# Four transformer layers on one core: the first four weight units taken by halves, with the products of the low weights last

## What is computed

```python
hn = rmsnorm(h, norm_mix[0])                  # h = x, [256, 1024]
q, k, v = split(hn @ w_qkv, 3)                # w_qkv [1024, 3072]; 8 heads of 128 channels
a = softmax(q0 k0^T * s + alibi) - lam * softmax(q1 k1^T * s + alibi)
o = rmsnorm(a @ v, subln) * (1 - lam_init)    # h = h + o @ w_o, then a SwiGLU FFN and a gated side input
```

## Time and profile before

| | us |
|---|---|
| median of 3 runs | 1311.12 (1311.06 to 1311.26) |
| the profiled execution | 1310.98 |
| its span, first to last instruction | 1309.2 |
| PE busy in it | 1299.0 (99%) |
| ACT busy | 847.5 (65%) |
| DVE busy | 963.5 (74%) |
| POOL busy | 114.8 (9%) |
| 16 DMA engines, bytes | 255.27 MB |

### The profile page before, as it was taken

The page is one execution under the profiler, slowest core; times in us unless marked ns, Lnnn a source line. Parts: engine busy times, 40 slices in busy tenths (PEclk is TensorE's granted clock), DMA queues, the critical chain, the costliest instruction groups (busy, mean ns, idle before and its releaser), DMA issues.

```text
span 1309.2 us, 20022 instructions
## 1 busy us (share of the span) xinstructions
PE 1299.0 (99%) x6642; PEld 1082.7 (83%) x6642; DVE 963.5 (74%) x1661; ACT 847.5 (65%) x1459; POOL 114.8 (9%) x163
## 2 busy tenths in 40 slices
PE   9999999999999999999999999999999999999998
PEld 7988888888888788888888888888887778888887
DVE  7877777676898676666699876666677887666664
ACT  7666666656788666665677666666578666666654
POOL 4020233410000000000010000000002210000000
PEclk9999999999999999999999999999999999999999
DMA  9454788876497556667647656676655545666661
GB/s 339 143 163 132 229 241 240 240 227 201 164 233 202 153 183 210 209 209 218 204 145 206 179 183 191 211 212 206 207 163 184 175 130 166 196 207 212 209 225 49
DMA packets 205055, 255.27 MB, mean 195 GB/s; under 512 B 72962, under 2 KB 163249, under 8 KB 204992
## 3 DMA queue, kind: packets, MB, share of 16 engines
q1 hardware_dynamic: 201984, 245.42, 60.6%
q0 software_dynamic: 2832, 8.49, 2.8%
q10 hardware_dynamic: 176, 0.54, 0.2%
HBM read 238.33 MB, written 1.13 MB: 183 GB/s over the span
## 4 chain that ended last, share of the span: by engine, by line
PE 93%; DVE 3%; ACT 1%; issue 1%; DMA 1%; POOL 0%; SPq 0%; DVEq 0%; ACTq 0%
PE acc L1620 15%; PE acc L1622 14%; PE acc L1621 14%; PE sc L1622 12%; PE sc L1620 12%; PE sc L1621 12%; PE turn L1781 3%; PE acc L1731 3%; PE acc L1733 3%; PE acc L1732 3%; PE turn L1883 1%; PE sc L1834 1%; DVE wlo L1139 1%; DVE z L1239 1%; PE turn L1863 1%
## 5 line engine op out<-in xcount | busy, mean ns | idle before, releaser
L829 ACT ACTIVATE whi<-raw,aT_gain 128x512 fp32r<-128x512 f32 (+2 forms) x612 | 403.8, 719 | 79.5 <-PE sc L1622 53.4
L1139 DVE SCALAR_TENSOR_TENSOR wlo<-raw,aT_gain,whi 128x512 fp32r<-128x512 f32 (+2 forms) x612 | 433.7, 764 | 28.6 <-ACT whi L829 24.5
L1620 PE MATMUL sc<-whi,xhi 128*128 128x512 f32 x640 | 249.4, 390 | 0.0
L1622 PE MATMUL sc<-whi,xlo 128*128 128x512 f32 x640 | 249.0, 389 | 0.0
L1621 PE MATMUL sc<-wlo,xhi 128*128 128x512 f32 x640 | 249.0, 389 | 0.0
L1620 PE MATMUL acc<-whi,xhi 128*128 128x512 f32 x432 | 173.2, 401 | 1.5 <-DVE wlo L1139 1.1
L1622 PE MATMUL acc<-whi,xlo 128*128 128x512 f32 x432 | 168.6, 390 | 0.0
L1621 PE MATMUL acc<-wlo,xhi 128*128 128x512 f32 x432 | 168.4, 390 | 0.0
L829 ACT ACTIVATE whi<-raw 128x1024 fp32r<-128x1024 f32 x120 | 125.9, 1055 | 63.5 <-PE acc L1622 56.9
L1137 DVE TENSOR_TENSOR wlo<-raw,whi 128x1024 fp32r<-128x1024 f32 x120 | 148.7, 1271 | 0.0
L1622 PEld LDWEIGHTS sc<-whi,xlo 128*128 128x128 f32 x640 | 120.1, 188 | 25.0
(11 more groups left out here) (213 smaller groups left out, 1965.9 us busy)
## 6 DMA issues: line engine op xcount, KB each, us to landing
raw<-in_ffn_w_gu SPq DMA_DIRECT2D x176, 256.0 KB
raw<-in_qk SPq DMA_DIRECT2D x62, 512.0 KB
raw<-in_ffn_w_gate SPq DMA_DIRECT2D x88, 256.0 KB
raw<-in_ffn_w_up SPq DMA_DIRECT2D x88, 256.0 KB
raw<-in_ffn_w_down SPq DMA_DIRECT2D x44, 512.0 KB
raw<-in_ffn_w_d SPq DMA_DIRECT2D x44, 512.0 KB
raw<-in_ple_w_gate SPq DMA_DIRECT2D x32, 512.0 KB
raw<-in_da_w_qkv SPq DMA_DIRECT2D x8, 512.0 KB
```

The lines of the kernel that those rows point to most:

```text
L829: ins = act.activation(whi[:, u % RING, c0:c1], raw[:, u % RING, c0:c1], ACT.Copy, scale=scale)
L1139: ins = dve.scalar_tensor_tensor(out=lo, in0=w, scalar=gain[:, g:g + 1], in1=hi.bitcast(F32), op0=ALU.mult, op1=ALU.subtract)
L1620: pe.matmul(dst, xh, wh, start=first, stop=False)
L1622: return pe.matmul(dst, xl, wh, start=False, stop=last)
```

## The change

- Units 2 and 3 are loaded and split by halves too (`HALVED` = 4), so the first four units are eight loads of 256 KB. x's first part is split as two single blocks (`X_SPLITS`); its loads stay as they were.
- PE takes units 0 to 3 in `first_unit`: for each half, both products of whi with xhi, then both of whi with xlo; at the end of the unit the four products with wlo. The count of matmuls is the same (12). Each kind waits for its own operand alone.
- `spin(9)` in place of `spin(13)`.
- x's rows are loaded behind units 4 and 5, no longer behind 3 and 4. ACT squares row tile 0 behind its split of unit 4 and tile 1 behind that of unit 5.
- DVE's split of unit 3 moves from ahead of the loop into step 0 (in the same place of its order: the splits of x stand ahead of it).
- Group 0's attention, from turnqk on, comes one step later (turnqk at s = 6, scores0 at s = 7, and so on to turno behind unit 15). evacqk stays. The norm factors' turn moves from s = 6 to s = 8. The other groups keep their steps.

The diff, cut to what the steps speak of:

```diff
--- before.py
+++ after.py
@@ -58,23 +58,25 @@
 
 
 X_PARTS = [(0, 2), (2, 4), (4, 6), (6, 8)]
-ROWS_BEHIND = {3: 0, 4: 1}
-
-
-def x_part(kb):
-
-    return [n for n, (k0, k1) in enumerate(X_PARTS) if k0 <= kb < k1][0]
+X_SPLITS = [(0, 1), (1, 2), (2, 4), (4, 6), (6, 8)]
+ROWS_BEHIND = {4: 0, 5: 1}
+HALVED = 4
+
+
+def x_split(kb):
+
+    return [n for n, (k0, k1) in enumerate(X_SPLITS) if k0 <= kb < k1][0]
 
 
 
 def splits(u):
 
-    return u + 1 + min(u + 1, 2)
+    return u + 1 + min(u + 1, HALVED)
 
 
 def landed(u):
 
-    return 32 * (u // RING + (u % RING > 1))
+    return 32 * (u // RING + (u % RING >= HALVED))
 LO_AHEAD = AHEAD - 1
 
 U_QKV = 0
@@ -165,6 +167,8 @@
         r = s - GROUP_UNITS * j - QK_UNITS
         if L == L_FX and j == 0 and r > 0:
             r = r if r == 1 else r - 1 if r > 2 else -1
+        if L == L_DA and j == 0 and r > 0:
+            r = r - 1 or -1
         if 0 <= r < len(tables[L]) + 3:
             names = tables[L][r] if r < len(tables[L]) else []
             if L == L_DA and j == HG - 1 and r >= LAST_PV:
@@ -217,7 +221,7 @@
 DVE_LEAD = RING + LO_AHEAD
 
 
-RS_SLOT = 6
+RS_SLOT = 8
 ACROSS = count([(L, j, b) for L in range(LAYERS) for j in range(HG) for b in range(2)
                 if across(L, j) and split_scores(L)])
 
@@ -398,7 +402,7 @@
 
         weights_in = [sem(f"weights_in{i}") for i in range(RING)]
         iota_ready, dist_ready = sem("iota_ready"), sem("dist_ready")
-        part_in = [sem(f"part_in{i}") for i in range(4)]
+        part_in = [sem(f"part_in{i}") for i in range(2 * HALVED)]
         hi_done, lo_done, unit_done = sem("hi_done"), sem("lo_done"), sem("unit_done")
         acc_done = sem("acc_done")
         bank_out = [sem(f"bank_out{b}") for b in range(4)]
@@ -564,7 +568,7 @@
                         load_x(u)
                     if L == 0 and u > RING:
                         load_misc(u - RING - 1)
-                    if u < 2:
+                    if u < HALVED:
                         for k in range(2):
                             sp.dma_start(raw[:, u, 512 * k:512 * k + 512], a["qk"][0, 0, b, :, 512 * k:512 * k + 512])\
                                 .then_inc(part_in[2 * b + k], 16)
@@ -980,19 +984,15 @@
 
             def split_x(n):
 
-                k0, k1 = X_PARTS[n]
-                act.wait_ge(x_t_in[n], 16)
+                k0, k1 = X_SPLITS[n]
+                act.wait_ge(x_t_in[k0 // 2], 16)
                 act.activation(xhi[:, k0:k1, :], x_block(k0, k1), ACT.Copy).then_inc(x_t_hi, 1)
 
-            for u in range(2):
-                split_x(u)
+            for u in range(HALVED):
                 for k in range(2):
+                    if u == 0 or k == 0:
+                        split_x(x_split(2 * u + k))
                     split_part(u, k)
-            for b in (2, 3):
-                split_x(x_part(2 * b))
-                split(b, unit_parts(0, b))
-            act.wait_ge(x_in[0], 16)
-            norm(0, 0, [0])
             for L in range(LAYERS):
                 base = UNITS * L
                 for s in range(U_FFN):
@@ -1008,9 +1008,9 @@
                         if (L, name, j) != (0, "evacqk", 0):
                             attention(L, name, j)
                     split_ahead(L, s)
-                    if (L, s) == (0, 0):
-                        act.wait_ge(x_in[1], 16)
-                        norm(0, 0, [1])
+                    if L == 0 and s < T:
+                        act.wait_ge(x_in[s], 16)
+                        norm(0, 0, [s])
                     for name, j in steps(ACT_STEPS, L, s, "behind"):
                         attention(L, name, j)
                     if L == 2 and s == 1:
@@ -1150,7 +1150,10 @@
 
             def split_ahead(L, s):
                 u = UNITS * L + s + LO_AHEAD
-                if u < LAYERS * UNITS:
+                if u < HALVED:
+                    split_part(u, 0)
+                    split_part(u, 1)
+                elif u < LAYERS * UNITS:
                     split(u, unit_parts(u // UNITS, u % UNITS))
 
             def lo_half(label, lo, hi, src, e, turns=0, per=0):
@@ -1436,18 +1439,17 @@
             dve.memset(ones_sb[:, :], 1.0).then_inc(consts, 1)
             def split_x(n):
 
-                k0, k1 = X_PARTS[n]
+                k0, k1 = X_SPLITS[n]
                 dve.wait_ge(x_t_hi, n + 1)
                 dve.tensor_tensor(xlo[:, k0:k1, :], x_block(k0, k1), xhi[:, k0:k1, :].bitcast(F32), ALU.subtract)\
                     .then_inc(x_t_lo, 1)
 
-            for u in range(2):
-                split_x(u)
+            for u in range(HALVED):
                 for k in range(2):
-                    split_part(u, k)
-            split_x(x_part(4))
-            split(2, unit_parts(0, 2))
-            split_x(x_part(6))
+                    if u == 0 or k == 0:
+                        split_x(x_split(2 * u + k))
+                    if u < HALVED - 1:
+                        split_part(u, k)
             for L in range(LAYERS):
                 base = UNITS * L
                 for s in range(U_FFN):
@@ -1685,11 +1687,36 @@
                     if t == 0:
                         behind()
 
+            def first_unit(u):
+
+                for k in range(2):
+                    kb, w = 2 * u + k, whi[:, u, 512 * k:512 * k + 512]
+                    pe.wait_ge(x_t_hi, x_split(kb) + 1)
+                    pe.wait_ge(hi_done, kb + 1)
+                    for t in range(T):
+                        pe.matmul(acc[t][:, :], xhi[:, kb, t * P:(t + 1) * P], w, start=kb == 0, stop=False)
+                    pe.wait_ge(x_t_lo, x_split(kb) + 1)
+                    for t in range(T):
+                        pe.matmul(acc[t][:, :], xlo[:, kb, t * P:(t + 1) * P], w, start=False, stop=False)
+                last = u == QK_UNITS - 1
+                for t in range(T):
+                    for k in range(2):
+                        kb = 2 * u + k
+                        if t == 0:
+                            pe.wait_ge(lo_done, kb + 1)
+                        ins = pe.matmul(acc[t][:, :], xhi[:, kb, t * P:(t + 1) * P], wlo[:, u, 512 * k:512 * k + 512],
+                                        start=False, stop=last and k == 1)
+                    if last and t == 0:
+                        ins.then_inc(acc_done, 1)
+                ins.then_inc(unit_done, 1)
+
             def qkv_unit(L, s):
 
                 u, j, b = UNITS * L + s, s // GROUP_UNITS, s % GROUP_UNITS
-                if u > 1:
-                    ready(u)
+                if u < HALVED:
+                    first_unit(u)
+                    return
+                ready(u)
                 half = b >= QK_UNITS
                 if not half and across(L, j):
                     across_unit(L, s, j, b)
@@ -1704,10 +1731,6 @@
                         pe.wait_ge(bank_out[bank], outs(bank, L, j))
                     for k in range(2):
                         cols = slice(512 * k, 512 * k + 512)
-                        if u < QK_UNITS and t == 0:
-                            pe.wait_ge(x_t_lo, x_part(2 * u + k) + 1)
-                        if u < 2 and t == 0:
-                            pe.wait_ge(lo_done, 2 * u + k + 1)
                         ins = three(acc[bank][:, :], xhi[:, kb + k, t * P:(t + 1) * P],
                                     xlo[:, kb + k, t * P:(t + 1) * P], whi[:, u % RING, cols],
                                     wlo[:, u % RING, cols], first and k == 0, last and k == 1)
@@ -1917,7 +1940,7 @@
                     pe.matmul(sc[:, 0, 0:P], ident[:, :], ident[:, :], start=True, stop=True)
 
             pe.wait_ge(consts, 2)
-            spin(13)
+            spin(9)
 
             for L in range(LAYERS):
                 def h_start(q, L=L):
```

## The result

| | before | after |
|---|---|---|
| median of 6 runs each, us | 1311.09 (1310.72 to 1311.31) | 1315.95 (1314.85 to 1316.98) |
| the profiled execution, us | 1310.98 | 1314.85 |
| its span, us | 1309.2 | 1313.0 |

The ratio is 1.0037 [1.0027, 1.0048]: the kernel is 4.86 us slower, where I had forecast 1.3 us faster. The profiled execution is of the lower level; what makes the upper one is shown with the last runs.

The account below looks back on a forecast made before the run. TensorE (PE) was taken to bound the kernel, with 93% of the chain. Gains of 0.95 us at scores0 and 0.3 us up to step 16 made 1.25, hence a median of 1309.8 us; 8-in-10 range 1308.4 to 1311.1.

Parts of the forecast that it names:

- Parts 1 and 2: Warm-up and units 0 to 3: first product at 5.54, 0.5 us lost to slow products, the 1.13 us wait gone.
- rival E: Units 0 to 3: real products come before the clock has risen, it stays at 1.2 GHz; 1317.2 us, chance 0.04.
- Part 3: x's rows one load later: unit 4 starts at 17.05, 2.28 us earlier; evacqk stays at about 20.7, no price.
- rival C: Halves of units 2 and 3 load slowly, later landings 1.2 us later, scores0 at 29.3; 1311.1 us, chance 0.06.
- the estimate of up to 4 us: Rule against the forecast: two further transfers cost up to 4 us without overlap, the change slower by about 3 us.
- Part 4: Group 0's attention one step later: PE waits 1.6 us for DVE's turnqk split, scores0 at 28.10, gain 0.95 us.
- rival A: At scores0 PE does not wait, DVE being through turnqk by 26.5; gain up to 3.0, 1308.2 us, chance 0.11.
- Part 5: From scores0 up to step 16: 0.3 us more gained, then the shift stays to the end.
- The 0.3 ahead of turnp0: Ahead of group 1's turnp0: DVE's old lateness goes, 0.3 us gained, bounds 0 and 0.45.
- Rival B: Steps 8 to 12: DVE piled up, taking back gain until 0 to 1 us is left; 1310.1 to 1311.1, chance 0.16.
- Rival D: Ahead of scores0: the clock falls to 1.2 GHz in the 1.6 us idle time, costing 2.4 us; 1312.2, chance 0.03.

Follow-up runs that it names:

- the halves alone: The changed kernel with group 0's attention and the norm factors' turn back at their old steps: 1310.96 us, ratio 1.0000 against before.
- the first try at the bank: The changed kernel with group 0's turno one more step later, behind unit 16: 1313.43 us, ratio 1.0018 against before.

## Why the prediction was wrong

Against my -1.25 the profiled execution has +3.84 at the end of its span, and the median +4.86.

- **Parts 1 and 2** held in what happens: 5.46 for 5.54, three slow products, no wait in units 0 to 3, so rival E did not come. The slow start cost 0.9 us, not 0.5. Unit 4 came at 17.35, not 17.05, 0.3 late, because PE and not the landing set it: its own products fill 5.46 to 17.35. Part 2's "end at about 16.8" is a slip: its own terms, 5.54 + 48 x 0.23 + 0.5 + 0.2, give 17.3. (In the same way E's 48 products at 0.43 end at 26.2 and not 26.0, and 1309.73 + 0.14 is 1309.9.) None of these moves the forecast of scores0, which DVE set.
- **Part 3** held: POOL's factors ended at 20.61 (20.5) and evacqk stood at 20.79 (20.7). Units by halves did not load more slowly (unit 4 landed about 14.3, 14.2 forecast), so rival C did not come. The advice of the Trainium skill's page "DMA: Bandwidth & Descriptors", section "Rules for kernel authors", to move at least 1 MiB with each DMA did not matter here: by that landing, transfers of 256 KB cost nothing that shows. The fixed 2.0 us behind the estimate of up to 4 us is given in its section "Anatomy of one DMA" for transfers that GpSimd issues, and these loads are issued by SP. (The ratio 1.0000 of the halves alone says little on this, since their gain is lost at the transposes in any case.)
- **Part 4** held in its mechanism (one wait ahead of scores0, ended by DVE's split, so no rival A) and was 0.46 short in size: a wait of 1.85 for 1.6, scores0 at 28.56 for 28.10, gain 0.49 for 0.95. DVE's chain ran late: unit 8 ended at 26.63 for 26.3, lambda at 27.09 for 26.67, turnqk at 28.42 for 27.96.
- **Part 5, the banks.** The 0.3 ahead of turnp0 came (0.37). I had gone through DVE's and ACT's load for steps 8 to 16 but not through what PE waits for before it writes, the bank. My sum has no term for it. It cost 1.54 us, so that layer 0 ends at +0.68 instead of -1.25. Rival B is the nearest to it (DVE late ahead of step 16), with another place and a loss I had held at 1 us at most.
- **Part 5, "from there on PE's work and its rings are the same and the shift stays to the end"** is the step that failed most. I had written "the change acts" only in the first 60 us and read the slot as layer 0's, while its condition holds for three layers. It cost 3.16 us in this profile, 2.9 to 3.1 in the runs that isolate it. No view of the first 60 us can show it. A search for every place where `RS_SLOT` is read, or the rows of line 1470 (three of them, 27.9 to 674.5), would have.
- **Rival D** is real. I gave it 0.03, on the ground that an idle time of 1.13 us had not lowered the clock. By their times it happened in six of eight executions of after; in the one of them whose trace is at hand it cost 1.4 us (0.213 - 0.120 for 15 steps), not 2.4.
- The sum as measured: -1.25 forecast, +0.39 at scores0 and turnp0, +1.54 bank, +3.16 slot, gives +3.84; +1.1 for the level at which most executions lie gives the median's +4.86 to within 0.1. By the bounds that I had set (slower above 1313.7) the result lies where I gave 0.05, and not by the mechanism that I had for it, rival E. Without the bank and the slot the change ends at -0.5 (1310.57), at the upper edge of the 1309.0 to 1310.6 that my forecast gave.

## What to carry to other kernels

When a constant is changed, list every layer and every loop that reads it before deciding which stretch of the profile to read. When a step moves in a hand-written order, redo the list of who shares a buffer by parity with whom, because a swap of two neighbours gives a third one a new and later reader. And when an engine works ahead of another, moving the producer later costs the reader its lead and all that is queued behind it, even where both still meet their own deadlines; the order in which a loaded engine takes two ready items (here 1.9 us) may be worth as much as the time won in front of it (here 1.98 us at unit 4).

## What was unexpected of the hardware

TensorE's clock can fall after an idle time of 1.8 to 1.9 us. The fall shows in the granted clock (0.51 from 30.2 to 33.4 us), and it did not come in the idle time but 1.6 us after work had resumed at 28.56 (in the first try at the bank 0.7 us after, 29.4 against 28.69); it ended while PE was busy. It costs 1.4 us and comes in some executions of one and the same kernel; in 11 executions with the idle time filled by matmuls whose result is not used it did not show. The slow start, on the other hand, does not show in the granted clock: it reads 1.00 from 1.5 to 5.5 us of before, where the matmuls of the warm-up start 0.21 us apart, as at 1.2 GHz, and not 0.11. The Trainium skill, in the page "TensorE: Matmul & The Clock Gate", section "A second HAM failure mode: psum-queue depth-cycling", describes a kernel in which TensorE idles briefly between groups of matmuls, often enough that its clock goes back and forth between the full and the half rate. The rows here show the same two rates, but behind a single idle time; repeated short ones were not tried.
